# Two-layer mLSTM, convolution and expert trunk: rows spread over the partitions and gate rows formed by GpSimd, head-norm weight as a column, two of layer 2's weight loads moved, and the output gate's sigmoid finished on ScalarE

## The chip, the cores and the metric

The kernel runs on one core of a Trainium2 chip. Its time is device microseconds (us) of one execution. TensorE (PE) multiplies matrices into the eight PSUM banks, VectorE (DVE) and ScalarE (ACT) do elementwise work, GpSimd (POOL) can also work across partitions, and SyncE (SP) issues most DMA transfers. All arrays are fp32, and the activations, 256 tokens, stay on the chip; the weights, some 297 MB, are read once from HBM.

## What is computed

The reference, cut to what matters (two layers, width 1024, 256 tokens, 4 groups of 4 experts):

```python
cond = silu(c)
for l in range(DEPTH):
    mod = cond @ w_ada[l] + b_ada[l]
    sh1, sc1, gt1, sh2, sc2, gt2 = split(mod, 6)
    u = x * (1 + sc1) + sh1
    q, k, v, o, i_pre, f_pre, cb, cc, ch = split(u @ w_in[l])
    h = mlstm_chunkwise(q, k, v, i_pre, f_pre)
    h = head_norm(h, mh_norm_w[l]) * sigmoid(o)
    y_conv = cb * causal_conv3(cc * ch, w_conv[l])
    mix = concat(h, y_conv) @ w_out[l]
    x = layer_norm(ALPHA * x + (1 + gt1) * mix, ln1_g[l], ln1_b[l])
    u = x * (1 + sc2) + sh2
    y = hier_moe(u, ...)          # top group, then top 2 of its 4 experts
    x = layer_norm(ALPHA * x + (1 + gt2) * y, ln2_g[l], ln2_b[l])
```

The two gates gt1 and gt2 are needed as rows over the width, the same on all 128 partitions, because tokens lie on the partitions where they are used.

## The kernel before

**Weights.** Six ring slots of 2 MB and a seventh, `bench`, hold the weights. The table `STREAM` writes the order of the mixers' loads by hand: `ada` units (512 columns of `w_ada`, numbered 0 to 11 per layer; 4, 5, 8, 9 are shift and scale for the experts, 6 and 7 gate 1, 10 and 11 gate 2), `proj` units 0 to 6 (512 columns of `w_in`) and two `wout` units. After them come 48 expert loads per layer, six for each of 8 pairs of experts. A load takes the slot of the load six places ahead of it in the ring and is issued by SP, in order, when that one has been used (L415, L364). Expert load 6 of each layer is the first to use `bench`, which holds the weighed sums and partial results in the mixer; SP holds it for `row_ext` (the last gate-row matmul). Load 7 waits for the first expert slot to come free.

**The condition's product.** VectorE computes `cond @ w_ada` by weighing: `ada_weigh(l, i)` multiplies the eight 128-row chunks of unit i by a scalar per partition and adds them up, eight instructions of 128x512 (L1139, L1141). What is left is the sum over partitions. TensorE forms it with a matrix of ones: `four_sums` (L573) and four transposes, `four_columns` (L580), give shift and scale as columns, which `moe_shift_scale` reads; `gate_row_half` (L568) gives a gate row on all partitions, to which VectorE (`gate_rows`, L1154, L1157) adds 1 and the bias, loaded by GpSimd's DMA as a row repeated for 128 partitions (L452). Gate 1 and gate 2 share one tile `gate_row`, and gate 2's sums take gate 1's place in `bench`.

**GpSimd** otherwise only makes constants and issues such spread loads: norm weights and offsets `ln_g`, `ln_b` (512 KB each), the head norm's weight `mh_w`, the routing biases, and the routing weights (`load_route`).

**The mixer.** TensorE projects block by block (L652 channels, L669 tokens) out of four banks. VectorE does the gates' prefix sums, the exponents' arguments, the head norm and the convolution; between them it weighs. The output gate's sigmoid is exp(-o) on ScalarE (L1048), then add 1 and reciprocal on VectorE (L1473, L1474). At the end TensorE transposes the heads (L866), projects the last block, forms sums and gate rows, and runs the output projection (L889) in four blocks of 128 tokens x 512 columns, while `first_norm` on VectorE multiplies by the gate row (L1259) and adds. Routing follows, then the pairs: gate (L696), up (L696), transpose, down (L720), combine. `down_copy` (L1376) multiplies by gate 2's row. `stay_busy` puts matmuls of zeros (L536) where TensorE would stand idle.

## Time and profile before

| | |
|---|---|
| median of 3 runs | 819.16 us (817.65 to 821.26) |
| the profiled execution | 819.95 us |
| its span, first to last instruction | 818.1 us |
| granted TensorE clock, mean | 0.994 of full speed |
| TensorE, VectorE, ScalarE, GpSimd busy | 97%, 52%, 12%, 4% of the span |
| read from HBM | 297.63 MB, 365 GB/s over the span |

Busy shares are averages over stages. Layer 1's mixer reaches to about 188 us, its experts to about 418 us, layer 2's mixer to about 578 us, its experts to the end. Durations below come from the profiled execution. "Idle before <-X" in a row is how long the engine stood before the instruction and what it waited for.

### The profile page before, as it was taken

The page shows a single profiled execution, that of the slowest core. Times are in us where ns is not written, and L with a number is a line of the kernel's source. Part 1 is how long each engine was busy: PE and PEld are TensorE (multiplying, and loading weights), DVE is VectorE, ACT ScalarE, POOL GpSimd, SP SyncE. Part 2 cuts the span into 40 slices and gives each one's busy share as a digit, 9 for nine tenths or more (in the row PEclk, how much of TensorE's full clock was granted, in tenths as well). Part 3 has the DMA queues.
Part 4 walks back from the last instruction along what each step waited for, and adds up shares of the span by engine and source line. Part 5 has one row for each costly group of instructions (what it writes and reads, how often), then busy time and mean ns, then how long its engine had stood idle before and what let it go on. Part 6 is the DMA issues. An engine that isn't in the chain of part 4 may idle for free.

```text
span 818.1 us, 9332 instructions
## 1 busy us (share of the span) xinstructions
PE 790.1 (97%) x3834; PEld 425.7 (52%) x3834; DVE 425.1 (52%) x916; ACT 96.0 (12%) x217; POOL 28.7 (4%) x72
## 2 busy tenths in 40 slices
PE   7999999999999999999979999999999999999994
PEld 2585588465344434434337658856634444443431
DVE  0289889787413332341356995676741343334135
ACT  2211000012011101101121101001201100110110
POOL 3000000520000000000001000000000000000000
PEclk9999999999999999999999999999999999999998
DMA  9999999899999999999998799547799999999991
GB/s 311 389 387 339 387 388 361 323 361 365 413 409 415 416 409 414 415 409 414 415 386 302 287 385 386 190 184 286 294 409 409 415 415 409 415 415 410 414 414 68
DMA packets 90826, 299.34 MB, mean 366 GB/s; under 512 B 4172, under 2 KB 4476, under 8 KB 82588
## 3 DMA queue, kind: packets, MB, share of 16 engines
q1 hardware_dynamic: 87132, 291.62, 91.7%
q0 software_dynamic: 2592, 7.04, 2.3%
q8 instruction: 33, 0.54, 0.3%
q10 hardware_dynamic: 1056, 0.03, 0.1%
q14 instruction: 13, 0.11, 0.0%
HBM read 297.63 MB, written 1.05 MB: 365 GB/s over the span
## 4 chain that ended last, share of the span: by engine, by line
PE 84%; DMA 6%; DVE 5%; issue 3%; ACT 1%; POOL 1%; DVEq 0%; POOLq 0%
PE bank L696 23%; PE bank L652 17%; PE bank L720 12%; PE bank L683 8%; PE bank L669 7%; DMA ring<-in_w_up_dram 6%; PE bank L742 4%; PE bank L889 3%; PE bank L536 2%; DVE bench L1141 1%; PE bank L551 1%; PE bank L568 1%; PE bank L704 1%; PE bank L750 1%; DVE expo L1141 1%
## 5 line engine op out<-in xcount | busy, mean ns | idle before, releaser
L652 PE MATMUL bank<-uT,ring 128*128 128x256 f32 x640 | 140.7, 380 | 0.0
L652 PEld LDWEIGHTS bank<-uT,ring 128*128 128x128 f32 x640 | 120.9, 190 | 19.3 <-issue 3.6
L696 PE MATMUL bank<-ring,uT 128*64 128x512 f32 x448 | 99.2, 594 | 1.8 <-DMA ring<-in_w_up_dram 1.8
L720 PE MATMUL bank<-ring,hb 128*64 128x512 f32 x448 | 99.6, 595 | 1.4 <-ACT hb L1012 1.4
L696 PE MATMUL bank<-ring,qT 128*64 128x512 f32 x448 | 99.4, 594 | 0.2 <-issue 0.2
L1141 DVE SCALAR_TENSOR_TENSOR bench<-ring,cond,bench 128x512 f32<-128x512 f32 x126 | 94.7, 752 | 4.5
L1376 DVE SCALAR_TENSOR_TENSOR kT<-bank,share,gate_row 128x512 f32<-128x512 f32 x32 | 24.0, 749 | 90.0 <-PE bank L720 90.0
L683 PEld LDWEIGHTS bank<-ccT,X 128*128 128x128 f32 x512 | 61.5, 197 | 11.3 <-issue 11.3
L696 PEld LDWEIGHTS bank<-ring,uT 128*64 128x64 f32 x448 | 31.6, 137 | 64.6 <-issue 60.0
L683 PE MATMUL bank<-ccT,X 128*128 128x128 f32 x512 | 64.3, 284 | 0.0
L720 PEld LDWEIGHTS bank<-ring,hb 128*64 128x64 f32 x448 | 30.9, 137 | 62.8 <-issue 60.5
L1363 DVE TENSOR_TENSOR o_sig<-o_sig,bank 128x512 f32<-128x512 f32 x16 | 11.0, 688 | 100.8 <-issue 80.0
L696 PEld LDWEIGHTS bank<-ring,qT 128*64 128x64 f32 x448 | 31.7, 137 | 59.2 <-issue 58.2
L669 PE MATMUL bank<-ring,uT 128*128 128x512 f32 x128 | 55.8, 594 | 0.0
L889 PE MATMUL bank<-ring,mixT 128*128 128x512 f32 (+1 forms) x160 | 55.3, 507 | 0.0
L889 PEld LDWEIGHTS bank<-ring,mixT 128*128 128x128 f32 x160 | 30.3, 190 | 24.5 <-issue 22.9
L742 PE MATMUL bank<-expo,hb 128*128 128x512 bf16 x168 | 41.0, 380 | 0.0
L669 PEld LDWEIGHTS bank<-ring,uT 128*128 128x128 f32 x128 | 24.0, 190 | 29.3 <-issue 29.3
L1008 ACT ACTIVATE o_sig<-bank 128x512 f32<-128x512 f32 x16 | 9.6, 597 | 215.2 <-PE bank L696 215.2
L1355 DVE TENSOR_SCALAR qT<-bank,mod 128x128 f32<-128x128 f32 x32 | 10.9, 404 | 42.0 <-PE bank L683 42.0
L1355 DVE TENSOR_SCALAR uT<-bank,mod 128x128 f32<-128x128 f32 x32 | 10.9, 405 | 40.6 <-PE bank L683 40.6
L742 PEld LDWEIGHTS bank<-expo,hb 128*128 128x128 bf16 x168 | 15.4, 98 | 24.8 <-issue 11.4
(278 smaller groups left out, 658.5 us busy)
## 6 DMA issues: line engine op xcount, KB each, us to landing
ring<-in_w_gate_dram SPq DMA_DIRECT2D x28, 2048.0 KB, 18.5
ring<-in_w_up_dram SPq DMA_DIRECT2D x28, 2048.0 KB, 19.6
ring<-in_w_down_dram SPq DMA_DIRECT2D x28, 2048.0 KB, 16.9
ring<-in_w_ada_dram SPq DMA_DIRECT2D x23, 2048.0 KB, 18.2
ring<-in_w_in_dram SPq DMA_DIRECT2D x14, 2048.0 KB, 17.9
ring<-in_w_out_dram SPq DMA_DIRECT2D x4, 2048.0 KB, 15.5
bench<-in_w_gate_dram SPq DMA_DIRECT2D x4, 2048.0 KB, 11.9
bench<-in_w_up_dram SPq DMA_DIRECT2D x4, 2048.0 KB, 18.7
```

Of the source, the lines that this page charges most:

```text
L536: pe.matmul(bank[bk][:, :], zeros[:, 0:P], zeros[:, :], start=True, stop=True)
L652: last = pe.matmul(bank[4 + (b0 + q) % 4][:, 0:SEQ], w[:, kc, q * P:(q + 1) * P], uT[:, kc, :], start=(kc == 0), stop=(kc == KC - 1))
L669: last = pe.matmul(bank[4 + (b0 + t) % 4][:, :], uT[:, kc, t * P:(t + 1) * P], w[:, kc, :], start=(kc == 0), stop=(kc == KC - 1))
L683: last = pe.matmul(bank[6 + kc // 4][:, (kc % 4) * P:(kc % 4 + 1) * P], X[:, t, rows_of(kc)], disp[b][:, t, :], start=(t == 0), stop=(t == ...
L696: last = pe.matmul(bank[bk][CAP * j:CAP * (j + 1), :], xg[b][:, 4 * h + k, CAP * j:CAP * (j + 1)], ring[s[h]][:, 4 * j + k, :], start=(h = ...
L720: last = pe.matmul(bank[6 + half][CAP * j:CAP * (j + 1), :], hhT[:, f, CAP * j:CAP * (j + 1)], ring[s[h]][:, 4 * j + 2 * i + half, :], sta ...
L742: last = pe.matmul(bank[2 * t + half][:, :], sent[b][:, t * P:(t + 1) * P], dn_parts[i][:, half * COLS:(half + 1) * COLS], start=False, st ...
L889: last = pe.matmul(to, mixT[:, kc, t * P:(t + 1) * P], w[:, kc, cols], start=(kc == 0), stop=(kc == KC - 1))
L1141: ins = dve.scalar_tensor_tensor(out=sums, in0=w[:, kc, :], scalar=cond[:, kc, 0:1], in1=sums, op0=ALU.mult, op1=ALU.add)
L1355: last = dve.tensor_scalar(xg[b][:, kc, :], bank[7][:, (kc - 4) * P:(kc - 3) * P], mod[:, 3, kc:kc + 1], mod[:, 2, kc:kc + 1], ALU.mult, A ...
L1363: dve.tensor_tensor(hh, sg, bank[5][:, :], ALU.mult).then_inc(S.hh, 1)
L1376: dve.scalar_tensor_tensor(out=dn[:, cols], in0=bank[6 + half][:, :], scalar=share[:, 0:1], in1=gate_row[:, cols], op0=ALU.mult, op1=ALU.m ...
```

## The change

- GpSimd forms the gate rows (`gate_half`): a DMA adds the bias into one partition of the weighed sums (to which `ada_weigh` has already added 1/128 per partition, which makes the 1 of 1 + gate), and one `partition_all_reduce` of 128x512 writes the row on all partitions. TensorE's gate-row matmuls and VectorE's `gate_rows` go; gate 2 has a tile of its own, in the memory of `v_ext`, so its reduces wait until the values have been used (`pv_done`).
- Norm rows and routing biases are loaded into one partition and spread by `partition_broadcast`. Layer 2's routing weights are loaded at the start of layer 2 and no longer in layer 1.
- The head norm's weight is loaded like the convolution's, as columns, and ScalarE applies it while it copies the transposed heads; the multiply by `mh_w` goes.
- ScalarE finishes the sigmoid as exp(-ln(1 + exp(-o))); the add and reciprocal on VectorE go.
- In layer 2, `ada` units 10 and 11 are loaded ahead of `proj` units 5 and 6, and weighed in the middle of the mixer.
- TensorE does the four transposes for shift and scale after the first block of the output projection.
- SP holds the first `bench` load for `gate_row_ready`, that is for both halves of gate 2's row.

```diff
-                  ("proj", 1, 3), ("ada", 1, 8), ("ada", 1, 9), ("proj", 1, 4), ("proj", 1, 5), ("proj", 1, 6), ("ada", 1, 10),
-                  ("ada", 1, 11), ("wout", 1, 0), ("wout", 1, 1)]
+                  ("proj", 1, 3), ("ada", 1, 8), ("ada", 1, 9), ("proj", 1, 4), ("ada", 1, 10), ("ada", 1, 11), ("proj", 1, 5),
+                  ("proj", 1, 6), ("wout", 1, 0), ("wout", 1, 1)]
...
-        w_conv_col = sb("w_conv_col", [P, DEPTH, 3 * CH])
+        w_conv_col = sb("w_conv_col", [P, DEPTH, 3 * CH + HEADS])
...
+        v_flat = sb("v_flat", [P, T * HEADS * (DK + 1)])
+        v_ext = v_flat[:, :].rearrange("p (t h d) -> p t h d", t=T, h=HEADS)
+        gate_moe = v_flat[:, 0:D]
...
-        early_sums = part[:, 0, :]
+        early_sums = tmp[:, :]
...
+            sp.dma_start(w_conv_rows[3 * CH:3 * CH + HEADS, :, :], mh_norm_w.rearrange("l (h p) -> h l p", p=P)).then_inc(cols_landed, 16)
...
-                            sp.wait_ge(row_ext, 4 * l + 4)
+                            sp.wait_ge(moe_sum, l + 1)
+                            sp.wait_ge(gate_row_ready, 4 * l + 4)
+                            if l == 0:
+                                sp.wait_ge(early_sum, 1)
...
-            def load_gate_row(l, which):
-                gt = (2, 5)[which]
-                pool.dma_start(gate_row[:, :], b_ada[l, gt * D:(gt + 1) * D].partition_broadcast(P)).then_inc(gate_landed, 16)
-            def load_head_weight(l):
-                pool.dma_start(mh_w[:, :], mh_norm_w[l].partition_broadcast(P)).then_inc(head_landed, 16)
-            def load_norm_rows(l, which):
+            def gate_half(l, which, half):
+                i = (GATE1, GATE2)[which] + half
+                sums = weighed_sums(l, i)
+                bias = b_ada[l, ADA_COL[i]:ADA_COL[i] + COLS].rearrange("(a n) -> a n", a=1)
+                pool.wait_ge(weighed, turn(l, i))
+                pool.dma_start(sums[0:1, :], bias, accum_op=ALU.add).then_inc(bias_added, 16)
+                pool.wait_ge(bias_added, 16 * (4 * l + 2 * which + half + 1))
+                row = (gate_row, gate_moe)[which]
+                pool.partition_all_reduce(row[:, half * COLS:(half + 1) * COLS], sums, P,
+                                          bass.bass_isa.ReduceOp.add).then_inc(gate_row_ready, 1)
+            def norm_rows(l, which):
                 g, b = ((ln1_g, ln1_b), (ln2_g, ln2_b))[which]
-                pool.dma_start(ln_g[:, :], g[l].partition_broadcast(P)).then_inc(rows_landed, 16)
-                pool.dma_start(ln_b[:, :], b[l].partition_broadcast(P)).then_inc(rows_landed, 16)
+                pool.dma_start(ln_g[0:1, :], g[l].rearrange("(a n) -> a n", a=1)).then_inc(rows_landed, 16)
+                pool.dma_start(ln_b[0:1, :], b[l].rearrange("(a n) -> a n", a=1)).then_inc(rows_landed, 16)
+                pool.wait_ge(rows_landed, 16 * (4 * l + 2 * which + 2))
+                pool.partition_broadcast(ln_g[:, :], ln_g[0:1, :], channels=P).then_inc(rows_spread, 1)
+                pool.partition_broadcast(ln_b[:, :], ln_b[0:1, :], channels=P).then_inc(rows_spread, 1)
...
+                    pool.memset(v_ext[:, :, :, DK:DK + 1], 1.0).then_inc(ones_back, 1)
+                    load_route(l)
+                norm_rows(l, 0)
+                for half in range(2):
+                    gate_half(l, 0, half)
                 if l == 0:
                     arrived(pool, "wout", l, 1)
-                load_norm_rows(l, 0)
-                if l == 0:
-                    for i in range(DEPTH):
-                        load_route(i)
-                    for i in range(1, DEPTH):
-                        load_gates(pool, i)
-                pool.wait_ge(x_ready, 2 * T * l + T)
-                load_gate_row(l, 1)
+                    load_route(l)
+                    load_gates(pool, 1)
+                pool.wait_ge(route_landed, 16 * 10 * (l + 1))
+                pool.partition_broadcast(b_route_row[:, l, :], b_route_row[0:1, l, :], channels=P).then_inc(route_spread, 1)
+                pool.wait_ge(pv_done, HEADS * (l + 1))
+                for half in range(2):
+                    gate_half(l, 1, half)
                 pool.wait_ge(seeded, l + 1)
-                load_norm_rows(l, 1)
+                norm_rows(l, 1)
...
-            def gate_row_half(l, i):
-                pe.wait_ge(weighed, turn(l, i))
-                pe.matmul(bank[4 + i % 2][:, :], ones[:, :], weighed_sums(l, i), start=True, stop=True).then_inc(row_ext, 1)
...
-                gate_row_half(l, GATE1)
-                gate_row_half(l, GATE1 + 1)
-                pe.wait_ge(moe_copied, l + 1)
-                four_columns(3, moe_sums, even_odd, moe_ext)
...
+                        if not (t or half):
+                            pe.wait_ge(moe_copied, l + 1)
+                            four_columns(3, moe_sums, even_odd, moe_ext)
...
-                gate_row_half(l, GATE2)
+                stay_busy(4, 4)
...
+                act.wait_ge(proj_act, 16 * l + 12)
+                link(act.activation(o_sig[:, :, :], o_sig[:, :, :], ACT.Ln, bias=1.0))
+                act.activation(o_sig[:, :, :], o_sig[:, :, :], ACT.Exp, scale=-1.0).then_inc(sigmoid_ready, 1)
...
-                    act.activation(mixT[:, 2 * b:2 * b + 2, :], bank[b][:, :].rearrange("p (h s) -> p h s", h=2),
-                                   ACT.Copy).then_inc(hT_copied, 1)
+                    for h in (2 * b, 2 * b + 1):
+                        last = act.activation(mixT[:, h, :], bank[b][:, h % 2 * SEQ:(h % 2 + 1) * SEQ], ACT.Copy,
+                                              scale=w_conv_col[:, l, 3 * CH + h:3 * CH + h + 1])
+                    last.then_inc(hT_copied, 1)
...
-                        ins = dve.tensor_scalar(sums, w[:, 0, :], cond[:, 0, 0:1], None, ALU.mult)
+                        gate = i // 2 in (GATE1 // 2, GATE2 // 2)
+                        ins = dve.tensor_scalar(sums, w[:, 0, :], cond[:, 0, 0:1], 1.0 / P if gate else 0.0, ALU.mult, ALU.add)
...
-                link(dve.tensor_scalar(o_sig[:, :, :], o_sig[:, :, :], 1.0, None, ALU.add))
-                link(dve.reciprocal(o_sig[:, :, :], o_sig[:, :, :]))
                 if l == 0:
                     ada_weigh(1, 1)
+                else:
+                    dve.wait_ge(gate_row_ready, 4 * l + 1)
+                    ada_weigh(l, GATE2)
...
-                    if l == 0 and q in (1, 2):
-                        ada_weigh(1, 2, 4 * (q - 1), 4 * q)
+                    if q in (1, 2):
+                        if l:
+                            dve.wait_ge(gate_row_ready, 4 * l + 2)
+                        ada_weigh(1, 2 if l == 0 else GATE2 + 1, 4 * (q - 1), 4 * q)
...
-                dve.wait_ge(head_landed, 16 * (l + 1))
-                dve.wait_ge(gate_landed, 16 * (2 * l + 1))
-                link(dve.tensor_tensor(hb[:, :, :], hb[:, :, :], mh_w[:, :].unsqueeze(1).to_broadcast([P, T, WM]), ALU.mult))
+                dve.wait_ge(sigmoid_ready, l + 1)
...
-                gate_rows(l, 0)
-                for i in (GATE2, GATE2 + 1):
-                    dve.wait_ge(row_ext, 4 * l + 2)
-                    ada_weigh(l, i)
-                    if i == GATE2:
-                        moe_shift_scale(l)
                 dve.wait_ge(gate_row_ready, 4 * l + 2)
+                if l == 0:
+                    ada_weigh(l, GATE2)
+                moe_shift_scale(l)
+                if l == 0:
+                    ada_weigh(l, GATE2 + 1)
                 first_norm(l)
...
-                gate_rows(l, 1)
...
-                        gate_row_2(l)
+                        dve.wait_ge(gate_row_ready, 4 * l + 4)
```

The engines' orders show three places. First TensorE at the end of layer 1's mixer, before: L573 are the four sums, L568 the gate rows, L580 the transposes for shift and scale, L889 the output projection.

```order
L573 MATMUL bank<-bench,ones 32x512 [waits hvar_ready,weighed]
L573 MATMUL bank<-bench,ones 32x512 x3
L568 MATMUL bank<-bench,ones 128x512 [waits weighed,proj_dve]
L568 MATMUL bank<-bench,ones 128x512 [waits weighed]
L580 MATMUL bank<-ident,expo 128x128 [waits moe_copied]
L580 MATMUL bank<-ident,expo 128x128 x3
L889 MATMUL bank<-ring,mixT 128x512 [waits landed4,hT_copied]
L889 MATMUL bank<-ring,mixT 128x512 x15
```

And now (L581, L588 and L894 are the sums, transposes and projection):

```order
L581 MATMUL bank<-bench,ones 32x512 [waits hvar_ready,weighed]
L581 MATMUL bank<-bench,ones 32x512 x3
L894 MATMUL bank<-ring,mixT 128x512 [waits landed4,hT_copied,proj_dve]
L894 MATMUL bank<-ring,mixT 128x512 x7
L588 MATMUL bank<-ident,expo 128x128 [waits moe_copied]
L588 MATMUL bank<-ident,expo 128x128 x3
L894 MATMUL bank<-ring,mixT 128x512 x8
```

The two gate-row matmuls are gone, and the projection's first eight stand ahead of the transposes. Next GpSimd in layer 1, from its last small loads of layer 2's gate weights on, before (L452 and L461, L462 are the spread rows):

```order
L383 DMA b_gates_col<-in_b_gates_dram 8x1
L384 DMA w_gates_sb<-in_w_in_dram 128x8x8
L452 DMA gate_row<-in_b_ada_dram 128x1024 [waits x_ready]
L461 DMA ln_g<-in_ln2_g_dram 128x1024 [waits seeded]
L462 DMA ln_b<-in_ln2_b_dram 128x1024
```

And now, from the same load on; L536 spreads the routing biases, L461 adds the bias to the weighed sums, L464 is the reduce into gate 2's tile (`v_flat`):

```order
L386 DMA w_gates_sb<-in_w_in_dram 128x8x8
L536 ISA b_route_row<-b_route_row 128x20 [waits route_landed]
L461 DMA bench<-in_b_ada_dram 1x16x32 [waits weighed,pv_done]
L464 ISA v_flat<-bench 128x512 [waits bias_added]
L461 DMA bench<-in_b_ada_dram 1x16x32 [waits weighed]
L464 ISA v_flat<-bench 128x512 [waits bias_added]
```

Where GpSimd issued one load it now has two loads and two reduces, one after another. Last SP in layer 2, from `proj` unit 4 on, before (in_w_in are `proj`, in_w_ada `ada`, in_w_gate, in_w_up, in_w_down expert loads):

```order
L415 DMA ring<-in_w_in_dram 128x8x512 [waits proj_done]
L415 DMA ring<-in_w_in_dram 128x8x512 [waits weighed] x2
L415 DMA ring<-in_w_ada_dram 128x8x512 [waits proj_done]
L415 DMA ring<-in_w_ada_dram 128x8x512 [waits weighed]
L415 DMA ring<-in_w_out_dram 128x8x512 [waits weighed]
L415 DMA ring<-in_w_out_dram 128x8x512 [waits proj_done]
L364 DMA ring<-in_w_gate_dram 128x4x1024 [waits proj_done] x2
L364 DMA ring<-in_w_up_dram 128x4x1024 [waits weighed] x2
L364 DMA ring<-in_w_down_dram 128x2x2048 [waits mix_done] x2
L364 DMA bench<-in_w_gate_dram 128x4x1024 [waits row_ext]
```

And now:

```order
L418 DMA ring<-in_w_in_dram 128x8x512 [waits proj_done]
L418 DMA ring<-in_w_ada_dram 128x8x512 [waits weighed] x2
L418 DMA ring<-in_w_in_dram 128x8x512 [waits proj_done]
L418 DMA ring<-in_w_in_dram 128x8x512 [waits weighed]
L418 DMA ring<-in_w_out_dram 128x8x512 [waits weighed]
L418 DMA ring<-in_w_out_dram 128x8x512 [waits proj_done]
L366 DMA ring<-in_w_gate_dram 128x4x1024 [waits weighed] x2
L366 DMA ring<-in_w_up_dram 128x4x1024 [waits proj_done] x2
L366 DMA ring<-in_w_down_dram 128x2x2048 [waits mix_done] x2
L366 DMA bench<-in_w_gate_dram 128x4x1024 [waits gate_row_ready,moe_sum]
```

The `ada` pair has moved ahead of the `proj` pair, the first expert loads wait for other units than before, and the bench load waits for GpSimd.

## Rows read from the trace of the kernel before

**Rows 1.** The page: engines' busy us, DMA tenths by slice, one costly group.

```profile
PE 790.1 (97%) x3834; PEld 425.7 (52%) x3834; DVE 425.1 (52%) x916; ACT 96.0 (12%) x217; POOL 28.7 (4%) x72
...
DMA  9999999899999999999998799547799999999991
...
L1008 ACT ACTIVATE o_sig<-bank 128x512 f32<-128x512 f32 x16 | 9.6, 597 | 215.2 <-PE bank L696 215.2
```

**Rows 2.** Timeline of PE, last pairs: start, us, line, what [idle before <-releaser].

```profile
400.56 3.65 PE L696 MATMUL bank<-ring,uT 128*64 128x512 f32 x16 [1.02 <-DMA ring<-in_w_up_dram]
...
789.93 3.65 PE L696 MATMUL bank<-ring,uT 128*64 128x512 f32 x16 [0.80 <-DMA ring<-in_w_up_dram]
```

**Rows 3.** Windows of 5 us: engines' busy us; last PEclk, DMA share, GB/s.

```profile
195.00:200.00 5.00, 5.00 (x29) 2.14 (x25) 4.79 (x9) 0.60 (x1) 0.00 (x0) 1.00 0.65 238
...
205.00:210.00 5.00, 5.00 (x26) 1.58 (x22) 0.00 (x0) 0.00 (x0) 0.00 (x0) 1.00 1.04 415
```

**Rows 4.** The chain that ended last, layer 1's mixer: start, us, what.

```profile
145.03 1.00 PE bank L573 x8
146.03 1.93 PE bank L568 x4
```

**Rows 5.** Timeline of DVE in layer 1.

```profile
85.25 1.95 DVE L1467 SCALAR_TENSOR_TENSOR expo<-bank,expo 128x384 f32<-128x384 f32 x4
...
145.14 0.42 DVE L1527 TENSOR_TENSOR mixT<-convT,bank 128x256 f32<-128x256 f32 x1 [1.99 <-PE bank L652]
147.20 1.47 DVE L1154 SCALAR_TENSOR_TENSOR gate_row<-bank,gate_row 128x512 f32<-128x512 f32 x2 [1.64 <-PE bank L568]
...
149.10 5.48 DVE L1141 SCALAR_TENSOR_TENSOR bench<-ring,cond,bench 128x512 f32<-128x512 f32 x7
...
161.04 0.68 DVE L1259 TENSOR_TENSOR tmp<-bank,gate_row 128x512 f32<-128x512 f32 x1
```

**Rows 6.** The chain that ended last, end of layer 2's mixer.

```profile
538.11 1.91 PE bank L568 x4
540.02 0.46 PE bank L580 x4
540.49 27.52 PE bank L889 x80
```

**Rows 7.** Timeline of SP: start, us with waits inside, transfer, xcount.

```profile
188.17 0.37 SPq L364 DMA_DIRECT2D bench<-in_w_gate_dram  x1
195.94 0.37 SPq L364 DMA_DIRECT2D ring<-in_w_gate_dram  x1
...
492.15 0.99 SPq L415 DMA_DIRECT2D ring<-in_w_ada_dram  x2
...
577.96 0.37 SPq L364 DMA_DIRECT2D bench<-in_w_gate_dram  x1
```

**Rows 8.** DMA issues, 140 to 215 us: xcount, KB each, us to landing.

```profile
bench<-in_w_gate_dram SPq DMA_DIRECT2D x1, 2048.0 KB, 9.0
...
gate_row<-in_b_ada_dram POOLq DMA_DIRECT2D x1, 512.0 KB, 9.1
...
w_route_sb<-in_w_router_dram POOLq DMA_DIRECT2D x8, 16.0 KB, 6.9
```

**Rows 9.** POOL: its timeline; last a group by form (busy us, mean ns).

```profile
153.20 0.53 POOL L461 DMA_DIRECT2D ln_g<-in_ln_g_dram  x1 [53.95 <-DMA ring<-in_w_out_dram]
...
160.23 0.71 POOL L471 DMA_DIRECT2D w_route_sb<-in_w_router_dram  x1
...
L446 POOL TENSOR_SCALAR_AFFINE_SELECT head_row<-head_row 4x512 f32<-4x512 f32 x1 | 0.6, 640 | 0.0
```

**Rows 10.** Timeline of DVE in layer 2.

```profile
477.39 1.95 DVE L1467 SCALAR_TENSOR_TENSOR expo<-bank,expo 128x384 f32<-128x384 f32 x4
...
506.74 0.16 DVE L1481 COPY den<-bank 128x2 f32<-128x2 f32 x1 [6.67 <-PE bank L855]
...
519.01 0.42 DVE L1504 TENSOR_TENSOR zT<-ccT,bank 128x256 f32<-128x256 f32 x1 [3.03 <-PE bank L652]
```

62 lines of the change are left out of this document (22 added, 40 removed).

## The prediction

> **What bounds the kernel now.** I read the page first: engines and DMA as a whole, then waits, stage by stage. TensorE is busy 97% of the span, and the DMA engines nearly all of it, except in two slices around 511 to 552 us [rows 1]. Two limits this close mean that a removed instruction or byte counts only where its own engine ends last, so I went stage by stage.
>
> In the expert loops TensorE sets the pace. It waits for a weight once per layer, in the last pair: 1.02 us and 0.80 us [rows 2]. The DMA engines are saturated there, at 415 GB/s [rows 3]; they fall behind TensorE a little with every load and use up the ring's lead at the very end. Their stream starts, for load 7 of the stage, when TensorE frees the first slot (195.94); between the bench load, issued at 188.17, and that one the engines idle a third of a window (share 0.65) [rows 3, 7].
>
> In the mixers TensorE's projections set the pace. At the end of layer 1's mixer the chain goes over TensorE's sums and gate-row matmuls (145.03 to 147.96) to VectorE [rows 4], and VectorE then works without a pause: the gate row, units 10 and 11 at 5.9 us each, then the norm's first multiply at 161.04 [rows 5]. In layer 2 TensorE stays the limit: gate-row matmuls 1.91, transposes 0.46, then 27.52 us of output projection [rows 6].
>
> **The change, part by part.** *Layer 1's mixer end.* VectorE is done with the convolution at 145.56 [rows 5]. It used to get its next weighing at 147.20 + 1.4 = 148.6. Now it starts at 145.6, if gate 1's row is there, and ends unit 10 at 151.5. But the columns that it then wants now come from TensorE behind the first block of the output projection: 146.03 [rows 4] + 27.52 / 4 = 6.9 + 0.46 [rows 6] = 153.4. That is a new wait of 1.9 us, with VectorE's unit 11 and all of the norm queued behind it. Shift and scale take 161.04 - 148.6 - 2 x 5.9 = 0.6 us, unit 11 another 5.9: the norm starts at 153.4 + 0.1 + 0.6 + 5.9 = 160.0 or 160.1 instead of 161.0. Gain **0.9 us**; 3.0 without the new wait.
>
> *Layer 2's mixer end.* The gate-row matmuls go (1.91), the transposes stay inside the projection's run: everything from 540.49 on comes 1.9 us sooner. Units 10 and 11 leave VectorE here, but TensorE's 27.52 us hid them: nothing. They now run before 506.74, where VectorE waited 6.67 us for TensorE, and in the waits of 3.03 us between the z products [rows 10]; each piece is 2.9 us, so they fit. Gain **1.9 us**. The first can slip if its load is late, but it takes the place of loads that were issued some 15 us before 492.15. Projection loads 5 and 6 are now issued at 492.15 [rows 7]; TensorE wants load 5 after the fourth head's product, some 2 us after 506.74, so it has 16 us; the bench load took 9.0 [rows 8]. Nothing; if the cover were gone, the excess over 16 us comes in full.
>
> *Bytes.* Eighteen transfers that spread a row over the partitions, up to 512 KB each, become single rows. In the saturated stretch that counts: two rows of 512 KB after load 7's start, 1.05 MB / 415 GB/s = 2.5 us in each layer. That is more than the 1.02 and 0.80 that TensorE waited [rows 2], so both waits go. Gain **1.8 us**, and no more, since behind them TensorE is the limit.
>
> *Sigmoid and head weight.* VectorE loses an add, a reciprocal and a multiply in each layer, all in stretches where it waits for TensorE (1.99 in layer 1 [rows 5], 6.67 in layer 2 [rows 10]): nothing. ScalarE gains two instructions of 1024 columns, by its 0.60 for 512 columns [rows 1] some 1.1 us each, and two more, smaller, copies under TensorE's last projection block; it is 12% busy and nothing is queued behind them but the head norm's root. The fill-in matmuls that replace TensorE's last gate rows take their time: nothing. One more small DMA on SP at the start: 0 to 0.4 us.
>
> *GpSimd.* This is the unknown. No row shows its cross-partition reduce of 128x512 or its broadcast. Lower bound: one pass over 512 columns, 0.64 us [rows 9]. Upper bound: 128 partitions one after another, 128 x 0.64 = 82 us. Halving the partitions takes seven passes, 7 x 0.64 = 4.5 us; I take R = 4.5, since 128 lanes in one 0.64 us pass is what the row shows, so it is nearer to a few passes than to a serial walk. A broadcast of 1024 columns is then 1.3 us at best and 9 by seven passes; none is waited for within 20 us.
>
> The Trainium skill's "GPSIMD Engine Reference", section "Cross-partition — where GPSIMD wins", gives 247.7 us for a partition-axis tensor_reduce of 128x2048. An estimate by that page is 62 us for 512 columns, and with it this kernel would take about 1,175 us. No row here has such a reduce.
>
> When is each row ready? Gate 1's sums are weighed by 85.3 in layer 1 [rows 5] and 477.4 in layer 2 [rows 10]; each half then costs a DMA of the bias, 6.9 to 9.1 us [rows 8], and R. In layer 1 both are ready by 85.3 + 2 x (6.9 + 4.5) = 108 at the latest, against 145.6: 37 us spare. In layer 2 the second is ready by 500, wanted at 515: enough. Gate 2 in layer 1 is the tight one, because SP now holds the first bench load, and every load behind it, until that row stands. GpSimd begins at 153.20, issues ten loads (the last at about 159.2; rows 9 give 0.53 to 0.71 each), waits 6.9 us for them [rows 8], so is free at 166.4; then twice (6.9 + 0.2 + R): the row stands at 180.6 + 2R = **189.6**. Before, SP issued that load at 188.17, and it landed 9.0 us later [rows 7, 8]. It may slip to about 191, by the idle third of the window, and by 2.5 - 1.0 = 1.5 us more before TensorE feels it at the layer's end: limit 192.4. So 189.6 costs nothing. In layer 2 gate 2 starts after 508.5 and stands by about 535, and the loads before the bench one are held until about 566: free. Its issue moves from 577.96 [rows 7] to about 567, which is worth nothing, as load 7 still waits for TensorE.
>
> **Sum.** 0.9 + 1.9 + 1.8 = 4.6 us. The profiled execution took 819.95 (span 818.1 and 1.85 around it), so it would take 815.3; it lies 0.8 above the median of 819.16, and against the median I forecast **814.6 us**.
>
> **Rivals.**
> (A) The forecast, its own range 812.5 to 817 for the uncertainty of the waits. Chance 0.55.
> (B) Gate 2's row is a little late in layer 1. With 9.1 for each bias DMA and R = 6: 166.4 + 2 x 15.1 = 196.6, 4.2 beyond the limit; 818.8. For it: the DMA queue is saturated at that time, and an accumulating DMA may take longer than any in rows 8. Against: 2.8 us of slack. 0.17.
> (C) The other side: R is large enough that SP holds the expert loads. Each us of R costs 2 us; from R = 5.9 it costs, from R = 8.2 on the kernel is slower than before. At R = 12 the row stands at 204.6, 12.2 beyond the limit: 814.6 + 12.2 = 826.8. For it: nothing is known of the operation. Against: the one-pass row. 0.13.
> (D) The reduce walks the partitions serially. With R = 82, layer 1's gate 1 comes at about 257 instead of 145.6 (+112) and gate 2 at about 450 against 304 (+146), layer 2 as much again: about 1,330 us. This is the behaviour of the page above. 0.03.
> (E) The two engines disturb each other. Layer 1's gate 2 reduces run at about 173.5 to 178 and 185 to 190, the first inside VectorE's unbroken stretch. If VectorE stood still during it, +4.5, and with layer 2's reduces beside VectorE's filled waits nothing is left: about 819; at half, 817. Rows here never show GpSimd computing beside VectorE. 0.12.
>
> The Trainium skill's "GPSIMD Engine Reference", section "Specifications", says that GpSimd shares its SBUF interfaces with VectorE, with contention for VectorE instructions that read two SBUF inputs. By that page the weighings, which read weights and sums, would be hit; it speaks for E. The trace has no row for it.
>
> **How the numbers follow.** The measurement of this kernel tells about 0.5% from no change: 815.1 and 823.3. A gives 0.36 faster, 0.19 same; B 0.03 and 0.14; E 0.12 same; C 0.02 same, 0.11 slower; D 0.03 slower. Together faster 0.39, same 0.47, slower 0.14. The range 812 to 820 takes A, B and E.
>
> **What would show it.** Right: no gate-row matmul between TensorE's sums and the output projection; a VectorE wait of about 2 us for the transposes in layer 1, none of VectorE's norm before 160; no TensorE wait for a DMA in either last pair; the first bench load at about 190 and 567; reduces of 3 to 6 us. Wrong: a bench load after 192.4 in layer 1; a longer VectorE instruction while GpSimd reduces; a wait of TensorE for projection load 5 in layer 2; or TensorE waits in pairs 1 to 3 of layer 1, which would mean that SP's queue was held.

## The result

The changed kernel takes **831.88 us** (median of 4 runs, 830.46 to 832.98) against 819.66 us (4 runs) for the kernel before on the same chip: 1.0129 times as long, 95% interval 1.0100 to 1.0158 (the two medians as they stand give 1.0149). The prediction was 814.6 us. The profiled execution took 831.52 us, its span is 829.8 us.

The page of the changed kernel, as in [rows 1]; the last line is the DMA queue that GpSimd issues to (packets, MB, share of 16 engines):

```profile
PE 788.8 (95%) x3814; PEld 425.3 (51%) x3834; DVE 413.0 (50%) x900; ACT 100.8 (12%) x225; POOL 70.2 (8%) x93
...
DMA  9994999796799999999999599872699999999991
...
q0 software_dynamic: 1216, 0.25, 0.2%
```

All that was to get less did so: TensorE 1.3 us, VectorE 12 us, the rows' bytes all but gone. But the first DMA slices point at where time went: the fourth is some 40% busy, in the kernel before 90% or more.

**The start.** Three more rows of the kernel before, from the timelines of GpSimd and TensorE (start, us, engine, line), then GpSimd's and TensorE's timeline of the changed kernel:

```profile
2.78 0.28 POOL L446 TENSOR_SCALAR_AFFINE_SELECT ident<-ident 128x128 f32<-128x128 f32 x1 [0.24 <-POOL head_row L484]
...
36.19 0.28 PE L628 MATMUL bank<-zeros 128*128 128x256 bf16 x1 [1.54 <-ACT uT L980]
...
422.32 1.29 PE L536 MATMUL bank<-zeros 128*128 128x512 bf16 x4 [4.07 <-issue]
```

```profile
13.03 0.28 POOL L452 TENSOR_SCALAR_AFFINE_SELECT ident<-ident 128x128 f32<-128x128 f32 x1 [10.49 <-issue]
...
26.92 1.30 POOL L473 PARTITION_BROADCAST ln_g<-ln_g  x1 [6.84 <-issue]
```

```profile
17.03 0.27 PE L802 MATMUL bank<-ident,expo 8*128 8x8 f32 x1 [12.44 <-POOL tmp L517]
...
47.78 0.28 PE L636 MATMUL bank<-zeros 128*128 128x256 bf16 x1 [1.54 <-ACT uT L987]
```

GpSimd's first affine_select starts 10.25 us later, after 10.49 us in which GpSimd waited for nothing that the profile shows. TensorE waits for those constants, and its granted clock then drops for a while (0.82 and 0.84 in the windows of 30 to 40 us, 1.00 in the same stretch before), so everything from 36.19 on is 11.6 us late. A second such gap, 6.84 us, stands in front of the first broadcast, where nobody waits.

**Layer 1's mixer end.** VectorE's timeline, then GpSimd's, then TensorE's:

```profile
165.19 0.17 DVE L1232 TENSOR_TENSOR scale<-bank,b_ada_col 128x8 f32<-128x8 f32 x1 [2.00 <-PE bank L588]
...
171.73 0.68 DVE L1253 TENSOR_TENSOR tmp<-bank,gate_row 128x512 f32<-128x512 f32 x1
...
176.79 0.69 DVE L1254 SCALAR_TENSOR_TENSOR X<-X,tmp 128x512 f32<-128x512 f32 x1
...
182.84 2.55 DVE L1254 SCALAR_TENSOR_TENSOR X<-X,tmp 128x512 f32<-128x512 f32 x1
```

```profile
182.61 3.24 POOL L464 PARTITION_ALL_REDUCE v_flat<-bench  x1 [4.21 <-DMA bench<-in_b_ada_dram]
...
191.32 3.23 POOL L464 PARTITION_ALL_REDUCE v_flat<-bench  x1 [4.77 <-DMA bench<-in_b_ada_dram]
```

```profile
188.68 1.73 PE L630 MATMUL bank<-ident,X 128*128 128x128 f32 x12 [2.89 <-DVE X L1274]
...
194.30 3.64 PE L912 MATMUL bank<-kT,ones 128*128 128x40 f32 x16
...
205.64 2.59 PE L691 MATMUL bank<-ccT,X 128*128 128x128 f32 x20 [0.20 <-DVE ccT L1323]
```

```profile
190.00:195.00 5.00, 4.22 (x46) 3.11 (x44) 4.40 (x14) 2.25 (x7) 3.23 (x1) 0.52 1.02 425
195.00:200.00 5.00, 4.78 (x21) 4.01 (x22) 1.70 (x7) 0.70 (x1) 0.00 (x0) 0.50 0.26 108
200.00:205.00 5.00, 5.00 (x23) 1.63 (x22) 1.88 (x11) 0.60 (x1) 0.00 (x0) 0.61 0.30 87
```

VectorE waits 2.00 us for the transposes, and its norm starts at 171.73 against 161.04 [rows 5]: 0.9 us sooner, once the 11.6 of the start are taken off. Up to here all is as forecast. Then an instruction that usually takes 0.69 us takes 2.55, 0.23 us after GpSimd's all-reduce began. TensorE, whose own work here has become shorter, stands idle for 2.89 us, and after that its granted clock is 0.50 to 0.61 (the lower of its two levels, 1.2 GHz, most of the time): the 16 matmuls of L912 take 3.64 us, 1.98 in the kernel before. The first gather of tokens for an expert starts at 205.64; before, it was at 188.10. Of these 17.5 us, 5.9 are new: 1.0 stands already at the first transposes (188.68 against 176.12), 5.0 come between them and the gather (16.96 us against 11.98).

A ledger of how far each place of TensorE lies behind the kernel before, from the two timelines, one profiled execution each:

| place | before | after | behind | change |
|---|---|---|---|---|
| start of layer 1's projections | 36.19 | 47.78 | 11.6 | +11.6 |
| layer 1's first gather | 188.10 | 205.64 | 17.5 | +5.9 |
| layer 2's first input transposes | 423.40 | 437.53 | 14.1 | -3.4 |
| layer 2's first norm transposes | 567.83 | 579.68 | 11.9 | -2.3 |
| end of the span | 818.1 | 829.8 | 11.7 | -0.2 |

### The profile page after: what moved, and what is told of

Its sections match the earlier page's. It is cut to its first block, busy times and chain, and to the rows that moved or that the text cites. A ratio compares the mean times of both kernels' runs of the same rounds, so it can differ in the third digit from the quotient of the medians.

```text
span 829.8 us, 9324 instructions
## 1 busy us (share of the span) xinstructions
PE 788.8 (95%) x3814; PEld 425.3 (51%) x3834; DVE 413.0 (50%) x900; ACT 100.8 (12%) x225; POOL 70.2 (8%) x93
## 4 chain that ended last, share of the span: by engine, by line
PE 83%; DMA 6%; DVE 5%; issue 4%; ACT 1%; POOL 1%; DVEq 0%; POOLq 0%
PE bank L704 22%; PE bank L660 17%; PE bank L728 12%; PE bank L691 8%; PE bank L677 7%; DMA ring<-in_w_up_dram 6%; PE bank L894 4%; PE bank L750 4%; PE bank L549 2%; PE bank L564 1%; PE bank L712 1%; ACT uT L987 1%; PE bank L758 1%; PE bank L912 1%; DVE expo L1154 1%
## 5 line engine op out<-in xcount | busy, mean ns | idle before, releaser
L1154 DVE SCALAR_TENSOR_TENSOR bench<-ring,cond,bench 128x512 f32<-128x512 f32 x126 | 100.1, 795 | 4.4
L1370 DVE SCALAR_TENSOR_TENSOR kT<-bank,share,v_flat 128x512 f32<-128x512 f32 x32 | 24.0, 749 | 92.3 <-PE bank L728 92.3
L894 PE MATMUL bank<-ring,mixT 128*128 128x512 f32 (+1 forms) x160 | 55.9, 508 | 0.0
L894 PEld LDWEIGHTS bank<-ring,mixT 128*128 128x128 f32 x160 | 30.1, 190 | 25.2 <-issue 22.0
L750 PE MATMUL bank<-expo,hb 128*128 128x512 bf16 x154 | 37.8, 379 | 2.2 <-issue 2.2
```

What stands on the lines that cost most here:

```text
L750: last = pe.matmul(bank[2 * t + half][:, :], sent[b][:, t * P:(t + 1) * P], dn_parts[i][:, half * COLS:(half + 1) * COLS], start=False, st ...
L894: last = pe.matmul(to, mixT[:, kc, t * P:(t + 1) * P], w[:, kc, cols], start=(kc == 0), stop=(kc == KC - 1))
L1154: ins = dve.scalar_tensor_tensor(out=sums, in0=w[:, kc, :], scalar=cond[:, kc, 0:1], in1=sums, op0=ALU.mult, op1=ALU.add)
L1370: dve.scalar_tensor_tensor(out=dn[:, cols], in0=bank[6 + half][:, :], scalar=share[:, 0:1], in1=gate_moe[:, cols], op0=ALU.mult, op1=ALU.m ...
```

## The experiments

**e1: where does the 10.49 us gap come from?** The changed kernel with one instruction more, GpSimd's last:

```diff
                 norm_rows(l, 1)
+            pool.iota(spare[:, :], pattern=[[1, 8]], base=1, channel_multiplier=0,
+                      allow_small_or_imprecise_dtypes=True)
```

> The changed kernel, with one tiny iota (128x8) as GpSimd's last instruction. GpSimd's iota and affine_select belong to one instruction library, its reduce and broadcast to another, and the changed kernel waits 10.49 us in front of its first affine_select. Theory T1 (what was resident at the end of the last execution must be replaced at the start of this one): with the iota the first library is resident when an execution ends, the wait in front of the first affine_select falls from 10.49 us to about 0.24 us, the first projection starts near 37.5 us instead of 49.1 us, and the time falls by 10 to 11.6 us, from 831.9 to about 820.5. The extra load lies behind 612 us, where GpSimd has nothing to do. Rival R1 (a program that uses two libraries loads the first one cold at every start): the wait stays at 10.5 us and the time at 831.9.

Measured: 817.88 us (10 runs, 813.86 to 824.97), against 820.72 for the kernel before on that chip: ratio 0.9977, 0.9948 to 1.0007. GpSimd's timeline, its first affine_select and its last instruction:

```profile
3.02 0.29 POOL L453 TENSOR_SCALAR_AFFINE_SELECT ident<-ident 128x128 f32<-128x128 f32 x1 [0.49 <-POOL head_row L497]
...
605.88 0.33 POOL L543 IOTA spare<- 128x8 f32 x1 [11.99 <-issue]
```

The gap has moved from the start of the execution to a place where it is free, in front of the iota. T1 holds, R1 falls: what counts is which library the *last* execution left behind. ("Library" is a name for what the gaps show: they stand between iota or affine_select on one side and reduce or broadcast on the other, never in front of a memset.) It gave 12.5 us by the two ratios (1.0129 and 0.9977) and 14.0 between the medians, the expected 11.6 and a little more. The profiled execution is the fastest of the ten: at layer 1's mixer end it had no held VectorE instruction (there the reduce took longer, 3.78 us), TensorE waited 1.44 us, and the clock stayed at 1.00.

**e2: the same cost alone.** The kernel before, with nothing of the change in it:

```diff
                 load_norm_rows(l, 1)
+            pool.memset(spare[:, :], 1.0).then_inc(const_step, 1)
+            pool.wait_ge(const_step, 29)
+            pool.partition_broadcast(spare[:, :], spare[0:1, :], channels=P)
```

> The kernel before, with nothing of the change but one broadcast over the partitions, of 8 columns, as GpSimd's last instruction, into a tile that nobody reads. T1: this alone costs the start of the next execution some 10.2 us in front of the first affine_select and the whole kernel 10 to 11.6 us, so 829.5 to 831. R1 gives the same, so it doesn't tell T1 from R1; both differ from a third theory R2 (the late start comes from something else in the change, such as the ninth small load at the start or the sums in another place): then it stays at 819.5.

Measured: 832.52 us, ratio 1.0153 (1.0113 to 1.0193). One broadcast of 8 columns, whose result nobody reads, over 200 us before the end:

```profile
12.97 0.28 POOL L447 TENSOR_SCALAR_AFFINE_SELECT ident<-ident 128x128 f32<-128x128 f32 x1 [10.44 <-issue]
...
614.00 0.28 POOL L532 PARTITION_BROADCAST spare<-spare  x1 [9.20 <-issue]
```

Between the medians it costs 11.8 us, about as much as the whole change lost (12.2). R2 falls.

**e3 and e5: TensorE's clock.** Fill-in matmuls on zeros where TensorE stood idle; e3 on e1's kernel, e5 on the changed kernel itself:

```diff
+                if l == 0:
+                    stay_busy(10, 4)
                 transpose_half(0, [(x_ready, 2 * T * l + 1)] * 2, rows_of, by_half)
+                if l == 0:
+                    stay_busy(3, 4)
                 transpose_half(1, [(y_ready, 2 * l + 1), (y_ready, 2 * l + 2)], rows_of, by_half)
```

> The kernel of e1 with 10 dependency-free 128x512 matmuls on zeros before TensorE's transposes of the first token half behind layer 1's output projection, and 3 before those of the second half, in stretches where TensorE stood idle for 2.89 and 0.78 us. The changed kernel loses 5.9 us between layer 1's output projection and its expert stage beyond the shift of the start. Theory T2 (two parts: GpSimd's all-reduce holds VectorE, 1.9 us, and TensorE, idle longer than before, then runs at the lower of its two clocks, about 4 us): the granted clock between 190 and 205 us of the old count stays near 1.0 instead of 0.5 to 0.6, the sums and transposes take 1.98 instead of 3.64, and the time is 3 to 4 us below e1, about 817. Rival (the clock falls for a reason other than TensorE's idle time, or the stretch is bound by VectorE): as e1, about 820.5.

> The changed kernel itself (without the iota at the end) with the fill-in matmuls of e3: 10 before TensorE's transposes of layer 1's first token half, 3 before those of the second. In the changed kernel's profile TensorE stood idle 2.89 us there and its granted clock then was 0.50 to 0.61 for 15 us; in e1, where the wait was 1.44 us, the clock stayed at 1.00. If the idle time brings the clock down: no window under 0.9 between 188 and 205 us, the first gather at about 200.5 instead of 205.6, and a time of about 827 to 828 instead of 831.9. Rival (the clock fell there for another reason, or by chance in that one execution): the median stays within 1.5 us of the changed kernel's 831.9.

Measured: e3 816.06 us (ratio 0.9944, 0.9925 to 0.9963), e5 826.86 us (4 runs, 825.58 to 829.40; ratio 1.0102, 1.0066 to 1.0138). The windows of e5:

```profile
190.00:195.00 5.00, 4.34 (x59) 3.53 (x57) 3.73 (x13) 2.57 (x6) 3.30 (x1) 1.00 1.01 423
195.00:200.00 5.00, 4.88 (x34) 2.34 (x33) 3.57 (x18) 0.72 (x2) 0.00 (x0) 1.00 0.45 152
200.00:205.00 5.00, 4.80 (x38) 4.14 (x38) 2.05 (x13) 2.49 (x6) 0.00 (x0) 1.00 0.97 379
```

The clock is 1.00 throughout and the first gather starts at 200.48 (expected 200.5), 5.2 us sooner. VectorE's instruction was held here too (2.17 us), and the first transposes start only 0.25 us sooner, so 4.9 us are the clock's. The size rests on the two profiles: the medians lie 5.0 us apart, the two ratios (1.0129 and 1.0102) only 2.2 us, with intervals that overlap, though none of e5's four runs (829.40 at most) is as slow as the changed kernel's fastest (830.46). The clock is not certain to fall, though. e1 had the same kind of wait, 1.44 us, and kept its clock in the profiled execution; e3's gain of 1.8 us over e1 is no more than the scatter, but its ten runs lie within 4.5 us of each other and e1's within 11.1.

**e4: the all-reduces out of VectorE's way.** Sums in tiles of their own, the first expert load free of GpSimd, layer 1's reduces behind the first selection matrix:

```diff
...
+            if i >= GATE2:
+                return gate2_sums[:, :] if i == GATE2 else dn[:, COLS:D]
-            return acc[:, (i - 4) if i < GATE2 else (i - 8), :]
+            return acc[:, i - 4, :]
...
-                            sp.wait_ge(gate_row_ready, 4 * l + 4)
+                            sp.wait_ge(gate_row_ready, 4 * l + 2)
...
+                if which and l == 0:
+                    pool.wait_ge(main.disp, 1)
```

> The kernel of e1, but the two weighed sums of the expert gate row lie in tiles of their own, so that the first expert load no longer waits for GpSimd, and layer 1's two all-reduces of them wait until the first selection matrix is built, which is behind VectorE's norm. T2: the VectorE instruction of 2.55 us is back at 0.69, TensorE's idle time before the transposes falls from 2.89 to about 1.0, its clock stays up, and all 5.9 us come back: about 814.5 to 816. Rival (the 5.9 us come from the gate row that stands late or from the expert load that GpSimd held, not from the two engines side by side): the load starts some 8 us sooner too, so the time would fall as well, but VectorE's 2.55 us and the low clock would stay. Second rival (the stretch stays slow whatever GpSimd does, as TensorE's clock falls at an idle time of 1 us as well): 1.9 us come back, 818.6.

Measured: 817.05 us (ratio 0.9958, 0.9935 to 0.9980), within the scatter of e1, and above the 814.5 to 816 expected. The norm's instruction is back at 0.69 us and TensorE waits 1.01 us, as expected, but the hold came along with the reduce to a place where it costs a little too:

```profile
188.40 2.10 DVE L1220 TENSOR_TENSOR mod<-mod,offset 128x8 f32<-128x8 f32 x1
...
194.75 2.02 DVE L1604 TENSOR_TENSOR comb<-chosen,dexp 128x32 f32<-128x32 f32 x1
```

An addition of 8 columns and a product of 32, 0.16 to 0.19 us at other times. The reduces began at 188.19 and 194.49.

**e7 and e8: how much does a reduce hold, and by what?** More all-reduces on e4's kernel, beside VectorE's unbroken stretch in layer 1; four of 512 columns in e7, eight of 64 (`range(8)`, `0:64`) in e8:

```diff
+                    pool.wait_ge(pv_done, HEADS)
+                    pool.wait_ge(gate_row_ready, 2)
+                    for k in range(4):
+                        pool.partition_all_reduce(v_flat[:, 0:512], gate_row[:, 0:512], P,
+                                                  bass.bass_isa.ReduceOp.add).then_inc(const_step, 1)
+                        pool.wait_ge(const_step, 29 + k)
```

> The kernel of e4 with four more all-reduces of 128x512, from a row that stands already into a tile that is dead, on GpSimd at about 161 to 175 us, beside VectorE's unbroken stretch at the end of layer 1's mixer. In the profiles so far one VectorE instruction that began 0.2 to 0.3 us after a reduce did took about 1.9 us longer (0.69 became 2.55, 0.16 became 2.10). Theory P (each reduce holds one VectorE instruction, once, for up to 1.9 us): four holds, VectorE's norm ends up to 7.6 us later and at least 4 us; the transposes at 180 to 184 instead of 176.1. Rival Q (the two engines share bandwidth, so that every VectorE instruction beside a reduce is a little longer): the instructions beside the reduces are all longer by a like share, none by more than double. Rival R (the holds are rare): transposes at 176 to 178.

> As e7, but eight all-reduces of 64 columns each. If a hold lasts as long as the part of the reduce that moves data, it shrinks with the columns: some 0.2 to 0.3 us for each, 2 us in all, transposes at about 178. If it is a fixed time per call: 8 x 1.9 us where each falls on VectorE, transposes at 185 or later. The reduce itself is expected at 0.4 to 0.6 us if it scales (3.23 us for 512 columns), or near 3 us if it doesn't.

Measured, one run each: 826.28 and 817.00 us. e7's GpSimd and VectorE:

```profile
162.63 13.16 POOL L544 PARTITION_ALL_REDUCE v_flat<-gate_row  x4
```

```profile
155.66 9.70 DVE L1168 SCALAR_TENSOR_TENSOR kT<-ring,cond,kT 128x512 f32<-128x512 f32 x7
165.28 0.68 DVE L1267 TENSOR_TENSOR tmp<-bank,gate_row 128x512 f32<-128x512 f32 x1
165.99 2.70 DVE L1268 SCALAR_TENSOR_TENSOR X<-X,tmp 128x512 f32<-128x512 f32 x1
168.73 0.75 DVE L1276 BATCH_NORM_STATS2 stats<-X 128x6 f32<-128x256 f32 x2
169.52 2.24 DVE L1166 TENSOR_SCALAR expo<-ring,cond 128x512 f32<-128x512 f32 x1
171.79 3.56 DVE L1168 SCALAR_TENSOR_TENSOR expo<-ring,cond,expo 128x512 f32<-128x512 f32 x2
```

and e8's:

```profile
163.54 6.94 POOL L544 PARTITION_ALL_REDUCE v_flat<-gate_row  x8
```

```profile
163.81 0.49 DVE L1166 TENSOR_SCALAR expo<-ring,cond 128x512 f32<-128x512 f32 x1
164.33 1.54 DVE L1168 SCALAR_TENSOR_TENSOR expo<-ring,cond,expo 128x512 f32<-128x512 f32 x2
...
166.63 0.71 DVE L1268 SCALAR_TENSOR_TENSOR X<-X,tmp 128x512 f32<-128x512 f32 x1
...
168.16 3.97 DVE L1168 SCALAR_TENSOR_TENSOR expo<-ring,cond,expo 128x512 f32<-128x512 f32 x5
```

In e7 the excess over the usual 5.48, 0.69, 0.49 and 1.54 us is 4.2 + 2.0 + 1.75 + 2.0 = 10.0 us, and the transposes start at 186.13 against e4's 176.10, 10.0 later. Each is one instruction. That is theory P in its form (one instruction per reduce is held, the rest, as the statistics and the product that reads a PSUM bank, take their time), but more than its 7.6, because the first is held for 4.2 us and not 1.9; no run shows why. Q falls. In e8 eight reduces of 512 columns in all take 6.94 us, 0.87 each, and hold VectorE for 0.1 us in all. The hold goes with the size of one call and nearly vanishes at 64 columns; the reduce itself scales only in part.

The profiles also show what sets the length of a hold. Wherever a reduce of 512 columns took its usual 3.2 to 3.3 us, the held instruction ended 2.0 to 2.1 us after the reduce's start plus its own usual time: 182.84 + 2.55 - 0.69 = 184.70 against 182.61 in the changed kernel, 188.40 + 2.10 - 0.17 = 190.33 against 188.19 in e4. One that begins later waits for less. In the changed kernel this one began 1.28 us into the reduce of 191.32 and took 0.97 us instead of 0.21:

```profile
192.60 0.97 DVE L1136 SCALAR_TENSOR_TENSOR nt<-rstd,var 128x1 f32<-128x1 f32 x1
```

The Trainium skill's "GPSIMD Engine Reference", section "Specifications", names as contended the VectorE instructions in a 2-port mode or with two SBUF inputs. Most held ones agree: the norm's sum reads X and tmp, the two of e4 read two tiles each. But e7's TENSOR_SCALAR of 169.52 reads one tile, and the changed kernel has one of 128x8 that takes 2.22 us instead of 0.17 beside the reduce of 527.56; the trace doesn't show whether they run in a 2-port mode. What the traces add is the size of the call.

**e6: the four transposes sooner.** In layer 1 behind the second matmul of the output projection instead of behind its first block (on e4's kernel):

```diff
+                                if l == 0 and not (t or half) and kc == 1:
+                                    pe.wait_ge(moe_copied, l + 1)
+                                    four_columns(3, moe_sums, even_odd, moe_ext)
                             last.then_inc(mix_done, 1)
-                        if not (t or half):
+                        if l and not (t or half):
```

> The kernel of e4 with TensorE's four transposes for layer 1's expert shift and scale moved from behind the first block of the output projection (8 matmuls) to behind its second matmul. VectorE's wait of 2.00 us for them should go. In e4 TensorE was done 1.01 us before VectorE at the end of this stretch, so it gives back 1.0 us and not 2.0: first transposes at about 175.1 instead of 176.1, time about 816.0 against e4's 817.05. Rival (TensorE waits for ScalarE's copy of the sums at the new place): no gain, and a TensorE wait for bank 3's copy inside the projection.

Measured: 817.29 us (ratio 0.9968, 0.9945 to 0.9990), no gain between medians. In its profile VectorE's wait is gone (the shift is computed at 153.25, the norm starts at 159.79) and TensorE goes from the projection into the transposes without a wait; from the start of layer 1's projections to the first gather it takes 186.91 - 37.93 = 149.0 us, in e4 188.16 - 37.07 = 151.1. The 2.1 us are lost again at the end of the expert stage, where TensorE stood 4.08 us for no shown reason; the other ten profiles without the large rows show 1.8 to 2.1 there.

**e9: every all-reduce in eight pieces of 64 columns** (on e4's kernel, without its delay):

```diff
-                pool.partition_all_reduce(row[:, half * COLS:(half + 1) * COLS], sums, P,
-                                          bass.bass_isa.ReduceOp.add).then_inc(gate_row_ready, 1)
+                for o in range(0, COLS, 64):
+                    ins = pool.partition_all_reduce(row[:, half * COLS + o:half * COLS + o + 64], sums[:, o:o + 64], P,
+                                                    bass.bass_isa.ReduceOp.add)
+                ins.then_inc(gate_row_ready, 1)
```

> The kernel of e4 with every all-reduce of 512 columns cut into eight of 64, and layer 1's no longer held back until the first selection matrix. e8 showed eight reduces of 64 columns in 6.94 us of GpSimd with no VectorE instruction beside them longer by more than 0.1 us; e7 showed four of 512 that cost VectorE 10.0 us. If the hold comes from the size of the one call, all of the changed kernel's long VectorE instructions go (weighing 7.33, 2.22, 2.03 and 2.55 us), and with them the two TensorE waits of 0.34 and 0.54 us that e4 has in its first expert pair: about 816 against e4's 817.05. If the hold comes from the two-input instructions of VectorE that e8 happened not to meet in the first microsecond, one or more instructions of over 1.5 us excess stay, and the time is 816 to 819.

Measured: 817.24 us (ratio 0.9956, 0.9933 to 0.9979), as e4. No VectorE instruction beside one of the 64 pieces is longer by more than 0.15 us, nor in e10 and e12. Of the 140 weighing additions the longest takes 1.69 us (usual 0.75, in the changed kernel up to 2.65), the next 1.53. Both stand beside the broadcasts of the norm's rows, GpSimd's timeline first, then VectorE's, and the changed kernel has the same two (1.60 and 1.53 us):

```profile
451.10 1.29 POOL L479 PARTITION_BROADCAST ln_g<-ln_g  x1 [2.38 <-DMA ln_b<-in_ln_b_dram]
452.25 1.70 POOL L480 PARTITION_BROADCAST ln_b<-ln_b  x1
```

```profile
449.53 5.62 DVE L1162 SCALAR_TENSOR_TENSOR bench<-ring,cond,bench 128x512 f32<-128x512 f32 x5
```

So the holds by the reduces are gone, and a broadcast of 1024 columns holds VectorE too, for 0.8 to 0.9 us. That the pieces save time could not be shown: e4 had lost under 1 us to the holds.

**e12: the pieces alone**, with the sums in the bench tile and the first expert load held until the row stands:

> The kernel of e1 (gate sums in the bench tile, first expert load held until the gate row stands) with the reduces cut into eight of 64 columns. No hold on VectorE, but the row stands 2 x 3.7 us later: at about 191 instead of 183.8, so the first load is issued at 191 instead of 185.6. The prediction's bound was that it may slip to about 192 before TensorE feels it. If that holds: no new TensorE wait for a weight in pair 1, time as e1 or 1 us less. Rival: TensorE waits 1 to 3 us for the loads of pairs 1 to 3 in layer 1 and the time is above e1 by as much.

Measured: 816.96 us (ratio 0.9952, 0.9930 to 0.9974). The row stands at 188.8 and the load is issued at 188.86, 3.3 us later than in e1 (185.57). TensorE waits for a weight once, 0.99 us in layer 2's last pair (e1: 0.17 in layer 1's, 0.55 in layer 2's), and not in layer 1; the median is not above e1's. So the 3.3 us cost nothing. But this is only 0.7 us later than in the kernel before (188.17), and the prediction's limit of 192.4 was not tried here.

**e11: the bytes.** The second norm's rows as 512 KB transfers again, on e1's kernel:

```diff
-                pool.dma_start(ln_g[0:1, :], g[l].rearrange("(a n) -> a n", a=1)).then_inc(rows_landed, 16)
-                pool.dma_start(ln_b[0:1, :], b[l].rearrange("(a n) -> a n", a=1)).then_inc(rows_landed, 16)
+                for t, row in ((ln_g, g[l]), (ln_b, b[l])):
+                    if which:
+                        pool.dma_start(t[:, :], row.partition_broadcast(P)).then_inc(rows_landed, 16)
...
```

> The kernel of e1 with one part undone: the second norm's two rows of each layer come again as DMAs that write all 128 partitions (512 KB each) in the expert stage, where the DMA engines are saturated, in place of a single row and a broadcast by GpSimd. In e1 TensorE waits 0.7 us for expert weights, in the kernel before 1.8 us. If the bytes are the reason, the wait returns to 1.6 to 2.0 us, the first input transposes of layer 2 come 1 us later relative to the first gather than e1's 231.9, and the time is 1 to 2 us above e1. Rival (the bytes are hidden, and e1's shorter expert stage has another cause): wait 0.7, stage 231.9, time as e1.

Measured: 820.98 us (ratio 1.0025, 0.9992 to 1.0058), 3.1 us above e1's median. The ten runs form two groups, six of 818.10 to 821.18 and four of 826.42 to 827.30 with a lower mean clock (0.979 to 0.981 against 0.989 to 0.991), and the interval overlaps with e1's, so the profiles decide. TensorE's timeline at the end of layer 1's expert stage, e11 and then e1:

```profile
401.99 3.65 PE L714 MATMUL bank<-ring,uT 128*64 128x512 f32 x16 [1.16 <-DMA ring<-in_w_up_dram]
...
423.78 1.49 PE L559 MATMUL bank<-zeros 128*128 128x512 bf16 x4 [4.10 <-issue]
```

```profile
399.36 3.65 PE L707 MATMUL bank<-ring,uT 128*64 128x512 f32 x16 [0.17 <-DMA ring<-in_w_up_dram]
...
419.15 0.81 PE L552 MATMUL bank<-zeros 128*128 128x512 bf16 x3 [2.10 <-issue]
```

From the first gather to layer 2's first input transposes e11 takes 235.5 us and e1 231.9; the kernel before 235.3, the changed one 231.9. So the two rows bring back the whole 3.4 us of the ledger. 1.0 is the longer wait for the weight, 2.0 the longer wait behind the stage's last matmuls, for which the profile names no cause, and 0.5 the fill-in matmuls behind it, which run at a lower granted clock (0.81 in the window of 423 to 425 us, in e1 1.00 at that place). One profile could be chance, as e6's 4.08 shows. But all three profiles with the large rows have the long wait (4.07 in the kernel before, 4.48 in e2, 4.10 in e11) and one of the eleven without them has it.

**e10: the terms together.** e9 with e6's place for the transposes and 2 and 1 fill-in matmuls:

> e9 with e6's place for the four transposes (behind the second matmul of the output projection in layer 1) and 2 and 1 fill-in matmuls ahead of layer 1's two runs of transposes. All the terms together: e9's 816 less 1.0 for the transposes' place, 815, and a narrower spread, since TensorE is idle under 0.5 us there. Rival: the terms overlap and it stands where e3, e4 and e6 stood, 816 to 817.3. Against the kernel before (about 820): 0.993 to 0.996.

Measured: **815.33 us** (9 runs, 811.23 to 817.76), the kernel before 821.50 (32 runs) on the same chip: ratio 0.9931, 0.9903 to 0.9959. It beats both kernels. TensorE no longer waits at all in front of layer 1's transposes:

```profile
174.89 0.59 PE L557 MATMUL bank<-zeros 128*128 128x512 bf16 x2
175.32 1.11 PE L638 MATMUL bank<-ident,X 128*128 128x128 f32 x8
```

## Why the prediction was wrong, step by step

**What failed first: a term that the sum doesn't have.** The prediction priced what GpSimd's new instructions take and when their rows stand. It allowed "0 to 0.4 us" for the start, for a small DMA, and did not ask what GpSimd must do before it can run them. By the gaps of e1 and e2, the reduce and the broadcast belong to another instruction library than the iota and the affine_select. Each switch took 6.8 to 13.2 us in the profiles, and since the changed kernel ends with the second library in place and begins with the first, one switch stands at the very start, where TensorE waits. That is +11.6 us; e2 shows it alone (+11.8), e1 shows it gone. The Trainium skill's "GPSIMD Engine Reference", section "Instruction dispatch", gives about 6 us for the first call to a freshly loaded kernel, without a visible instruction. Its sign agrees, and 6.84 us in front of the first broadcast is near it; the 10.49 us at the start are longer. By an estimate from that page's 6 us, one such load in front of TensorE's first wait would have taken away all of the forecast gain of 4.6 us.

**Rival E was right in kind and too cheap.** It had 0.12 and "VectorE stood still during it, +4.5", 819. The first reduce did fall into VectorE's unbroken stretch, and held it for 1.9 us, not for its whole length. But TensorE's clock, which the prediction did not price, followed: of the 5.9 us behind the start's shift, 5.0 come from the slower stretch behind the first transposes, and 4.9 of them went with the fill-ins of e5. The other 1.0 is what the hold took less what the mixer's end had gained (1.9 - 0.9).

**What was right.** Layer 1's mixer: VectorE's new wait 2.00 us (forecast 1.9), the norm 0.9 us sooner (0.9). Layer 2's mixer: -2.3 us from its input transposes to its norm's (forecast 1.9). Of these, 1.7 lie between its four sums and the norm's transposes, where the gate-row matmuls went, and 0.6 at its very start: there the kernel before ran at a granted clock of 0.50 to 0.65 from 423 to 427 us, behind its wait of 4.07 us, and the changed one at 1.00. So it is the forecast's mechanism at 1.7 us, and the rest belongs to that wait.

R: taken 4.5 us, measured 3.23 to 3.56. That it came near is luck: the row of 0.64 us behind it [rows 9] is an instruction on 4 partitions, not on 128, and nothing shows seven passes. With the bias DMAs at 5.1 and 5.6 us from issue to reduce instead of 6.9, gate 2's row stood at 194.55, 183.0 without the start's shift (forecast 189.6). The first expert load was issued at 202.46, 190.9 without the shift; it waited by then for the early sums, which TensorE made at the low clock, not for the row. TensorE waited for no weight in layer 1. In layer 2 that load went out at 580.35, some 568 without the shift (forecast 567). No reduce held SP; B, C and D did not happen.

**The bytes were undersized.** Forecast 1.8 us, 1.0 in layer 1 and 0.8 in layer 2. Measured 3.4 and 0.2. TensorE's waits for weights fell from 1.8 to 0.6 us: layer 1's went, layer 2's stayed at 0.60, against the sign that neither would be left. "1.8 us, and no more" did not hold either: a second wait at the end of layer 1's stage shrank too, from 4.07 to 2.08 us, and with it went the low clock behind it.

**Open.** Why TensorE waits there for 1.8 to 4.5 us; e6 had 4.08 without the large rows, so they are not the only cause. VectorE's norm is not all of it either: in the kernel before the first half of X stood at 421.12, and TensorE's next instruction began at 422.32. When exactly the clock falls after an idle time: 2.89 us did it in one profile, 1.44 us did not in another. At the end of layer 1's expert stage the four waits of 4.07 to 4.48 us were all followed by the lower clock, waits of 1.96 and 1.97 us in e4, e5 and e12 too, the same 1.97 us in e3 not. The scatter of single runs (11.1 us in e1) leaves 1 us effects between e4, e6, e9 and e12 undecided. VectorE's and ScalarE's shorter and longer lists (the sigmoid, the head weight) were forecast at nothing and not tried by themselves, nor was layer 2's order of loads; nothing in the ledger needs them.

Without the start's switch the change is worth 0.2% (e1, whose interval includes no change at all); with the reduces out of the way and TensorE kept busy, 0.7% (e10), which is what the prediction had hoped for the change as it stands (814.6 against 819.16, 0.56%).
